# Last dense block reordered by feature halves, first routing moved forward, row splits moved to GpSimd, routing steps joined

## The chip, the cores and the metric

One core of a Trainium2 chip runs the whole program in one launch. The metric is device time in microseconds of one execution, the median over runs. Engines are named as the profile names them: PE (matrix products), PEld (its weight loads), DVE (vector), ACT (scalar), POOL (GpSimd), SP (the queue that issues most DMAs).

## The reference, cut to what matters

One decoder layer on 512 tokens of 1024 features. Up to the place of the change it computes a mixer and its residual; after it come two experts out of 32 for each token, a gated embedding and a last norm.

```
h = h + merged @ w_out[l]                 # the last dense block
u = rms_norm(h, norm_ffn_g[l])
group_logits = uf @ w_rg + b_rg;  g_idx = argmax(group_logits)
exp_logits = (uf @ w_re + b_re).reshape(n, 4, 8);  sel = exp_logits[g_idx]
top_v, top_i = lax.top_k(sel, 2)
gates = p_group * softmax(top_v)
y = silu(xblk @ w_gate_e[e]) * (xblk @ w_up_e[e]) @ w_down_e[e]   # per expert
```

## The kernel before, in words

Tokens lie in four tiles ("rows" i = 0 to 3) of 128 tokens. The dense products are made with values split into a high and a low part: for one k tile of 128 features the high weights take two products (high and low data) and the low weights one. A dense tile of 128 by 512 over eight k tiles is 24 products. The k tiles come in two halves, g = 0 and 1, of 12 products each. Fifteen dense blocks of four tiles run in turn; the last two, `out`, make `merged @ w_out` for columns 0 to 511 and 512 to 1023, and their tiles are the four rows. DVE adds each finished tile to `h1` (`residual`, L1197).

From the last block on, each row also needs the following work, and every engine's order is written out by hand:

- PE: `transpose_h1(i)` (8 transposes, L1529, two banks), `scores(i)` (16 recorded products with `wrt`, the router weights), `logits(i)` (a fold of two halves with `fold`).
- ACT: `row_norm(i)` (square sum and root, L887, L888), `copy_row_half` (PSUM to `h1T`, L895), `copy_scores` (L905), `row_high(i)` (the row's high part for the later gather, L901, which reads `h1` with a step of eight elements).
- DVE: `rows_split(i)` (the low part, `h1 - rows_high`, L439, same step), `row_rstd(i)`, and for two rows at a time `route(half)`: the logits with the bias (`lg`, L1221), then three times `first_max` (maximum, equality, index, minimum, one-hot: L1208 to L1214), once for the group and twice for the expert. `find_places(half)` turns the counts of the product `places(half)` into `pick` (L1250), the matrix that gathers tokens.
- PE then gathers the rows of the first team of experts with `pick` (`gather_k`, 32 products for rows 0 and 1 and 32 for rows 2 and 3), ACT copies them, and the expert loop begins with `gate_or_up`. `keep_busy(n)` (L1481) is n small products with no use of their result.

SP loads expert weights into nine slots of 2 MB. Slots 5 to 8 overlap the last block's operands: their first halves are loaded after `first_half_used`, their second halves after the last block's last tile (`tile_done`). Everything after the ninth load waits for slots to come free: first for `part_used`, which `gate_or_up` raises a quarter into its first run of products. The expert loop uses 96 such loads.

In the last block, tile c = 4 + i has row i - 1's transposes before its second k half, the scores inside that half and the logits behind it. `route(0)` stands on DVE before the last tile's `residual`, and row 3 (and its transposes, scores, logits) follows the block.

Of the kernel before, what the change touches and what calls it, by code (L numbers as in the profile page):

```python
# [37 lines left out]
def build(nc, x, p, norm_mix_g, w_in, conv_w, conv_b, w_rg, b_rg, w_ig, b_ig, lru_lambda, w_pool, pool_scale,  # L38
# [54 lines left out]
    with ctx:  # L93
# [131 lines left out]
        iota = sb("iota", [P, C])  # L225
        fold = sb("fold", [P, NL])
# [425 lines left out]
        def _(pool):  # L652
            steps = 0

            def after(ins):
# [17 lines left out]
                           allow_small_or_imprecise_dtypes=True).then_inc(const_ready, 1)  # L673
            nc.gpsimd.iota(token[:, :], pattern=[[P, TT]], base=-FAR, channel_multiplier=1,
                           allow_small_or_imprecise_dtypes=True).then_inc(const_ready, 1)
            nc.gpsimd.memset(row_base[:, :], float(FAR)).then_inc(const_ready, 1)
            pool.wait_ge(const_ready, 7)
# [35 lines left out]
            low(5)  # L713

# [25 lines left out]
        def _(act):  # L740
# [166 lines left out]
            for i in range(TT - 1):  # L907
                act.wait_ge(h1_ready, TT + i + 1)
                row_norm(i)
                if i > 0:  # L910
                    row_high(i)
                copy_row_half(i, 0)
                copy_row_half(i, 1)
                if i == 0:
                    row_high(i)
                copy_scores(i)
# [3 lines left out]
            copy_scores(TT - 1)  # L920
# [139 lines left out]
        def _(dve):  # L1060
# [31 lines left out]
            dve.wait_ge(const_ready, 7)  # L1092
# [113 lines left out]
            def first_max(scores, n, best, index, cands, onehot):  # L1206
# [9 lines left out]
            def route(half):  # L1216
# [6 lines left out]
                first_max(lg[:, at, 0:NG], NG, t4[:, 0, at], t4[:, 1, at], g4[:, 1, at, :], g4[:, 2, at, :])  # L1223

                el_g = el[:, at, :].rearrange("p i (g e) -> p i g e", g=NG)
                after(v.tensor_scalar(g4[:, 1, at, :], g4[:, 2, at, :], 2 * BIG, -BIG, ALU.mult, ALU.add))
                after(v.tensor_tensor(el_g, lg[:, at, NG:NL].rearrange("p i (g e) -> p i g e", g=NG),
                                      g4[:, 1, at, :].unsqueeze(3).to_broadcast([P, 2, NG, PG]), ALU.min))
                first_max(el[:, at, :], NE, t4[:, 2, at], t4[:, 3, at], cand[:, at, :], oh1[:, at, :])
                after(v.scalar_tensor_tensor(out=el[:, at, :], in0=oh1[:, at, :], scalar=-2 * BIG, in1=el[:, at, :],  # L1230
# [22 lines left out]
            for t, (kind, c) in enumerate(tiles):  # L1253
# [31 lines left out]
                if ("out", c) == (kind, 2 * TT - 1):  # L1285
                    route(0)
                if kind == "out":
                    if TT < c < 2 * TT - 1:
                        rows_split(dve, c - TT - 1)
                    residual(c)  # L1290
# [3 lines left out]
                    if c > TT:  # L1294
                        row_rstd(c - TT - 1)
            find_places(0)
            dve.wait_ge(rows_psum, 2 * TT)
            dve.wait_ge(scores_psum, TT - 2)
# [158 lines left out]
        def _(pe):  # L1457
            def mm(*a, **k):
                return nc.tensor.matmul(*a, **k)  # L1459
# [406 lines left out]
```

## Time and profile before

| what | value |
|---|---|
| median of 3 runs | 885.79 us (885.78 to 886.18) |
| profiled execution, span from first to last instruction | 884.5 us |
| PE busy | 836.7 us, 95% |
| PEld busy | 527.9 us, 60% |
| DVE busy | 342.2 us, 39% |
| ACT busy | 273.0 us, 31% |
| POOL busy | 82.1 us, 9% |
| moved by DMA | 253.85 MB, mean 287 GB/s |

The span belongs to one profiled execution; the median is of other executions of the same program and is 1.3 us higher. Busy shares are averages over stages with different limits: the dense blocks (0 to 348 us), the change-over to the experts (348 to 364), the expert loop (to about 813) and the last norm and gate.

### The profile page before, as it was taken

Reading aid. Unit: us, or ns where it says so; the run is one execution under the profiler, and the core shown is the slowest. Engines: PE = TensorE matmul, PEld = TensorE weight load, DVE = VectorE, ACT = ScalarE, POOL = GpSimd, SP = SyncE. Lnnn points to the kernel's source line nnn. Section 1 sums busy time; section 2 is a strip of 40 time slices with the busy share of each in tenths; the row PEclk is TensorE's granted clock in tenths of the full one; section 3 lists DMA queues with packets and bytes.
Section 4 is the critical chain, followed back from the end, with each engine's and each line's share of the span. In section 5 each row is a group of like instructions: output and inputs, shape, how many; then the busy total and the mean of one; then the engine's idle time right before and its main releaser. Section 6 shows DMA issues by size and latency. Waiting matters only on the chain.

```text
span 884.5 us, 10432 instructions
## 1 busy us (share of the span) xinstructions
PE 836.7 (95%) x4321; PEld 527.9 (60%) x4321; DVE 342.2 (39%) x479; ACT 273.0 (31%) x401; POOL 82.1 (9%) x64
## 2 busy tenths in 40 slices
PE   5999999999999999999999999888998898999996
PEld 4888888788888887536535354352352352533685
DVE  6899549962651616511020120101100101015865
ACT  7666346733332226202010100101001001002777
POOL 3436380000000000000000000000000000001000
PEclk9999999999999999999999999999899999999999
DMA  9222222211525764899999999999999999998902
GB/s 260 97 93 96 95 96 96 96 49 49 189 96 207 296 257 179 349 423 425 401 428 426 428 426 429 426 428 428 428 428 428 426 425 430 427 421 347 356 2 95
DMA packets 45334, 253.85 MB, mean 287 GB/s; under 512 B 8868, under 2 KB 9960, under 8 KB 31976
## 3 DMA queue, kind: packets, MB, share of 16 engines
q1 hardware_dynamic: 42696, 248.21, 69.2%
q0 software_dynamic: 2304, 4.20, 1.2%
q8 instruction: 34, 0.56, 0.3%
q10 hardware_dynamic: 288, 0.79, 0.2%
q14 instruction: 12, 0.10, 0.0%
HBM read 246.89 MB, written 10.49 MB: 291 GB/s over the span
## 4 chain that ended last, share of the span: by engine, by line
PE 44%; DMA 14%; issue 1%; DVE 1%; ACT 1%; DVEq 0%; ACTq 0%
PE bank L1459 42%; DMA ring<-in_w_down_e_dram 11%; DMA ring<-in_w_gate_e_dram 3%; PE bank L1689 1%; PE bank L1785 0%; ACT L1046 0%; ACT r_rounded L901 0%; PE bank L1529 0%; DVE pick L1250 0%; DVE r_rounded L439 0%; ACT r L999 0%; ACT L999 0%; ACT junk L887 0%; PE bank L1775 0%; ACT gain L895 0%
## 5 line engine op out<-in xcount | busy, mean ns | idle before, releaser
L1459 PE MATMUL bank<-ring_rounded,ring_rounded 128*128 128x512 f32 (+1 forms) x696 | 245.0, 389 | 0.3 <-DVE ring_rounded L1134 0.3
L1459 PE MATMUL bank<-r_rounded,ring_rounded 128*128 128x512 f32 (+1 forms) x744 | 234.4, 389 | 0.7 <-DVE ring_rounded L1081 0.6
L1459 PEld LDWEIGHTS bank<-r_rounded,ring_rounded 128*128 128x128 f32 x744 | 138.9, 188 | 30.4 <-DVE ring_rounded L1081 0.9
L1459 PEld LDWEIGHTS bank<-ring_rounded,ring_rounded 128*128 128x128 f32 x696 | 130.3, 188 | 28.1 <-issue 1.3
L1459 PE MATMUL bank<-ring,gain 128*64 128x512 f32 x472 | 118.0, 604 | 9.3 <-issue 8.1
L1459 PE MATMUL bank<-ring,hT 128*64 128x512 f32 x400 | 112.3, 624 | 6.7 <-DMA ring<-in_w_down_e_dram 6.7
L1459 PE MATMUL bank<-ring,junk 128*64 128x512 f32 x472 | 115.5, 592 | 0.0
L1459 PEld LDWEIGHTS bank<-ring,gain 128*64 128x64 f32 x472 | 36.1, 138 | 76.3 <-issue 73.5
L1459 PEld LDWEIGHTS bank<-ring,junk 128*64 128x64 f32 x472 | 37.6, 137 | 71.4 <-issue 71.3
L730 POOL DMA_INDIRECT expert_rows<-r,row_i x16 | 16.5, 1032 | 669.3 <-DVE r L1346 669.3
L945 ACT ACTIVATE r<-bank,factor 128x512 f32<-128x512 f32 x16 | 11.0, 687 | 215.2 <-PE bank L1459 215.2
L1459 PEld LDWEIGHTS bank<-pick,r_rounded 128*128 128x128 f32 x576 | 71.1, 195 | 9.3 <-issue 8.5
L1459 PE MATMUL bank<-pick,r_rounded 128*128 128x256 f32 x576 | 73.1, 288 | 3.3 <-DVE pick L1250 3.3
L1346 DVE TENSOR_SCALAR r<-bank,factor 128x512 f32<-128x512 f32 x16 | 12.0, 751 | 156.3 <-PE bank L1459 156.3
L418 DVE TENSOR_TENSOR ring_rounded<-ring,ring_rounded 128x2048 fp32r<-128x2048 f32 x21 | 49.0, 2343 | 54.5 <-ACT ring_rounded L413 54.5
L1459 PEld LDWEIGHTS bank<-ring,hT 128*64 128x64 f32 x400 | 34.8, 143 | 54.0 <-issue 49.3
L413 ACT ACTIVATE ring_rounded<-ring 128x2048 fp32r<-128x2048 f32 x28 | 53.4, 1912 | 37.2 <-DMA ring<-in_w_in_dram 12.5
L1459 PE MATMUL bank<-ring_rounded,r_rounded 128*128 128x512 f32 (+1 forms) x152 | 57.0, 379 | 0.0
L940 ACT ACTIVATE sig<-bank,factor 128x512 f32<-128x512 f32 x16 | 11.0, 687 | 131.7 <-PE bank L1459 123.9
L1336 DVE SCALAR_TENSOR_TENSOR sig<-bank,factor,sig 128x512 f32<-128x512 f32 x16 | 12.0, 750 | 100.0 <-ACT sig L940 100.0
L1340 DVE SCALAR_TENSOR_TENSOR sig<-bank,factor,sig 128x512 f32<-128x512 f32 x16 | 12.0, 751 | 96.2 <-PE bank L1459 96.2
L1459 PE MATMUL bank<-r,hT 128*64 128x512 f32 x80 | 37.0, 618 | 4.8 <-DMA ring<-in_w_down_e_dram 4.8
(226 smaller groups left out, 761.6 us busy)
## 6 DMA issues: line engine op xcount, KB each, us to landing
ring<-in_w_up_e_dram SPq DMA_DIRECT2D x29, 2048.0 KB, 29.6
ring<-in_w_gate_e_dram SPq DMA_DIRECT2D x24, 2048.0 KB, 27.9
ring<-in_w_down_e_dram SPq DMA_DIRECT2D x22, 2048.0 KB, 32.0
ring<-in_w_in_dram SPq DMA_DIRECT2D x18, 1024.0 KB, 7.3
r<-in_w_gate_e_dram SPq DMA_DIRECT2D x5, 2048.0 KB, 27.9
r<-in_w_down_e_dram SPq DMA_DIRECT2D x4, 2048.0 KB, 34.2
ring<-in_w_down_e_dram SPq DMA_DIRECT2D x7, 1024.0 KB, 21.6
ring<-in_w_up_e_dram SPq DMA_DIRECT2D x6, 1024.0 KB, 11.0
```

What stands on the lines that cost most here:

```text
L413: nc.scalar.activation(high_half(n, h), whole_half(n, h), ACT.Copy).then_inc(high_ready, 1)
L418: api.tensor_tensor(low_half(n, h), whole_half(n, h), high_half(n, h), ALU.subtract).then_inc(low_ready[low_engine[n, h]], 1)
L730: nc.gpsimd.indirect_dma_start(out=y_rows, out_offset=bass.IndirectOffsetOnAxis(ap=row_i[:, m:m + 1], axis=0), in_=yrow(m), in_offset=None ...
L940: nc.scalar.activation(sig[:, :], bank[2][:, :], ACT.Sigmoid, scale=factor[:, m, 1:2]).then_inc(sig_ready, 1)
L945: nc.scalar.activation(yrow(m)[:, HALF:D], y_bank(m, 1)[:, :], ACT.Copy, scale=factor[:, m, 0:1]).then_inc(y_stored, 1)
L1336: v.scalar_tensor_tensor(out=sig[:, :], in0=bank[2][:, :], scalar=factor[:, m, 1:2], in1=sig[:, :], op0=ALU.mult, op1=ALU.mult).then_inc(g ...
L1340: v.scalar_tensor_tensor(out=sig[:, :], in0=bank[3][:, :], scalar=factor[:, m, 1:2], in1=sig[:, :], op0=ALU.mult, op1=ALU.mult).then_inc(h ...
L1346: v.tensor_scalar(yrow(m)[:, 0:HALF], y_bank(m, 0)[:, :], factor[:, m, 0:1], None, ALU.mult).then_inc(y_stored, 1)
L1459: return nc.tensor.matmul(*a, **k)
L1689: ins = nc.tensor.transpose(bank[3][:, k * P:(k + 1) * P], sig[:, :].rearrange("p (q k) -> p k q", k=KF)[:, k, :], ident[:, :])
```

## The change

- **Last block.** It was row by row. Now row 0 and row 1 are whole; then come row 2's first k half, row 3's first k half, and only then the second halves of rows 2 and 3. Transposes and scores of rows 0 and 1 and both their logits stand inside the block; rows 2 and 3 follow it together. `first_half_used` is raised after row 3's first half.
- **First routing.** `route(0)` begins before row 2's `residual`, which is placed in the middle of it (`meanwhile`).
- **ACT.** The scores of rows 2 and 3 are copied by one instruction of 256 columns; `row_high(2)` and `row_high(3)` follow it.
- **Row splits.** All four `rows_split` leave DVE for POOL, each waiting for `rows_high_ready` and for the one before.
- **Routing.** `first_max` needs no index subtraction: a table `falling` (32, 31, ...) is multiplied by the equality in one `scalar_tensor_tensor` per row, so two instructions in a row without a wait between them replace two chained ones. The masking of the experts is joined the same way.
- **Filler.** `keep_busy` 6, 14 becomes 4, 4, around the first gather.

The diff, cut:

```diff
-        def rows_split(dve, i):
-            dve.wait_ge(rows_high_ready, i + 1)
-            dve.wait_ge(rows_psum, 2 * i)
-            nc.vector.tensor_tensor(rows_low(i), h1_by_k(i), rows_high(i), ALU.subtract).then_inc(rows_low_ready, 1)
...
+            for i in range(TT):
+                pool.wait_ge(rows_high_ready, i + 1)
+                if i >= 1:
+                    pool.wait_ge(rows_low_ready, i)
+                    pool.wait_ge(rows_psum, 2 * i)
+                nc.gpsimd.tensor_tensor(rows_low(i), h1_by_k(i), rows_high(i), ALU.subtract).then_inc(rows_low_ready, 1)
...
+            act.wait_ge(scores_psum, TT)
+            nc.scalar.activation(hT[0:64 + NL, 1:3, :],
+                                 bank[0][0:64 + NL, (TT - 2) * P:TT * P].rearrange("p (i t) -> p i t", i=2),
+                                 ACT.Copy).then_inc(scores_ready, 1)
+            row_high(TT - 2)
             row_high(TT - 1)
...
                 after(v.tensor_reduce(best, scores, AX.X, ALU.max))
-                after(v.tensor_tensor(cands, scores, bc(best, n), ALU.is_equal))
-                after(v.scalar_tensor_tensor(out=cands, in0=cands, scalar=-float(C),
-                                             in1=iota[:, 0:n].unsqueeze(1).to_broadcast([P, scores.shape[1], n]),
-                                             op0=ALU.mult, op1=ALU.add))
-                after(v.tensor_reduce(index, cands, AX.X, ALU.min))
-                after(v.tensor_tensor(onehot, cands, bc(index, n), ALU.is_equal))
+                for i in range(2):
+                    ins = v.scalar_tensor_tensor(out=cands[:, i, :], in0=scores[:, i, :], scalar=best[:, i:i + 1],
+                                                 in1=falling[:, NE - n:NE], op0=ALU.is_equal, op1=ALU.mult)
+                after(ins)
+                after(v.tensor_reduce(index, cands, AX.X, ALU.max))
+                after(v.tensor_tensor(onehot, cands, bc(index, n), compare))
...
-            find_places(0)
-            dve.wait_ge(rows_psum, 2 * TT)
-            dve.wait_ge(scores_psum, TT - 2)
-            v.tensor_copy(h1T(TT - 1)[:, 4:8, :],
-                          bank[4 + (2 * TT - 1) % 3][:, :].rearrange("p (k t) -> p k t", k=4)).then_inc(last_rows_ready, 1)
-            rows_split(dve, TT - 2)
+            for i in (TT - 2, TT - 1):
+                dve.wait_ge(rows_psum, 2 * i + 2)
+                dve.wait_ge(scores_psum, i - 1)
+                v.tensor_copy(h1T(i)[:, 4:8, :],
+                              bank[4 + (2 * i + 1) % 3][:, :].rearrange("p (k t) -> p k t", k=4)).then_inc(last_rows_ready, 1)
             find_places(0)
+            row_rstd(TT - 2)
             row_rstd(TT - 1)
             route(1)
...
             find_places(1)
-            rows_split(dve, TT - 1)
...
+            products(row2, 0)
+            transpose_h1(1)
+            bank_free(row3)
+            products(row3, 0).then_inc(first_half_used, 1)
+            scores(1)
+            logits(0)
+            logits(1)
+            products(row2, 1).then_inc(tile_done, 1)
+            products(row3, 1).then_inc(tile_done, 1)
...
+            transpose_h1(TT - 2)
             places(0)
             transpose_h1(TT - 1)
-            keep_busy(6)
+            scores(TT - 2)
             scores(TT - 1)
+            logits(TT - 2)
             logits(TT - 1)
+            keep_busy(4)
...
-            keep_busy(14)
+            keep_busy(4)
             places(1)
```

Three places show how instructions move. On PE, between the last dense product and the first gather, before (`ident` marks a transpose of a row, `wrt` the scores, `fold` the logits, `routed_bf` the counting products):

```order
L1459 MATMUL bank<-routed_bf,ones 128x32
L1529 MATMUL bank<-ident,r 128x128 [waits rows_ready,h1_ready]
L1529 MATMUL bank<-ident,r 128x128 x3
L1529 MATMUL bank<-ident,r 128x128 [waits rows_ready]
L1529 MATMUL bank<-ident,r 128x128 x3
L1459 MATMUL bank<-before,ones 128x128 x6
L1459 MATMUL bank<-gain,wrt 36x128 [waits rows_ready]
L1459 MATMUL bank<-gain,wrt 36x128 x3
L1459 MATMUL bank<-gain,wrt 36x128 [waits last_rows_ready]
L1459 MATMUL bank<-gain,wrt 36x128 x3
L1459 MATMUL bank<-fold,hT 128x36 [waits scores_ready]
```

and with the change, behind the transposes of rows 2 and 3:

```order
L1542 MATMUL bank<-ident,r 128x128 [waits rows_ready]
L1542 MATMUL bank<-ident,r 128x128 x3
L1472 MATMUL bank<-r,wrt 36x128 [waits rows_ready]
L1472 MATMUL bank<-r,wrt 36x128 x3
L1472 MATMUL bank<-r,wrt 36x128 [waits last_rows_ready]
L1472 MATMUL bank<-r,wrt 36x128 x3
L1472 MATMUL bank<-gain,wrt 36x128 [waits rows_ready]
L1472 MATMUL bank<-gain,wrt 36x128 x3
L1472 MATMUL bank<-gain,wrt 36x128 [waits last_rows_ready]
L1472 MATMUL bank<-gain,wrt 36x128 x3
L1472 MATMUL bank<-fold,hT 128x36 [waits scores_ready] x2
L1472 MATMUL bank<-before,ones 128x128 x4
```

Only row 3 was left behind the block; now rows 2 and 3 are, and their two logits wait for one copy.

On POOL, from the last dense block's weight splits to the read of the number of rounds, before and with the change:

```order
L710 TENSOR_TENSOR r<-r 128x512 [waits pool_step]
L418 TENSOR_TENSOR ring_rounded_53<-ring,ring_rounded_52 128x2048 [waits high_ready,pooled]
L418 TENSOR_TENSOR ring_rounded_53<-ring,ring_rounded_52 128x2048 [waits high_ready]
L716 TENSOR_LOAD rounds_i [waits rounds_ready]
L716 ISA x2
```

```order
L419 TENSOR_TENSOR ring_rounded_53<-ring,ring_rounded_52 128x2048 [waits high_ready,pooled]
L419 TENSOR_TENSOR ring_rounded_53<-ring,ring_rounded_52 128x2048 [waits high_ready]
L717 TENSOR_TENSOR r_rounded_60<-r,r_rounded_58 128x1024 [waits rows_high_ready]
L717 TENSOR_TENSOR r_rounded_57<-r,r_rounded_58 128x1024 [waits rows_psum,rows_low_ready,rows_high_ready] x3
L720 TENSOR_LOAD rounds_i [waits rounds_ready]
```

POOL gets four instructions of 128 by 1024 that wait for ACT, ahead of its read of the rounds.

On DVE, between the first `pick` and the experts' first maximum in `route(1)`, before:

```order
L1250 TENSOR_TENSOR pick<-iota,place 128x512 [waits dve_chain]
L1299 COPY gain<-bank 128x512 [waits scores_psum,rows_psum]
L439 TENSOR_TENSOR r_rounded_57<-r,r_rounded_58 128x1024 [waits rows_psum,rows_high_ready]
L1201 RECIPROCAL rstd<-std 128x1 [waits row_std_done]
L1221 SCALAR_TENSOR_TENSOR lg<-bank,rstd,brt 128x36 [waits logits_psum,dve_chain]
L1221 SCALAR_TENSOR_TENSOR lg<-bank,rstd,brt 128x36 [waits dve_chain]
L1208 TENSOR_REDUCE t<-lg 128x2 [waits dve_chain]
L1209 TENSOR_TENSOR g<-lg,t 128x8 [waits dve_chain]
L1210 SCALAR_TENSOR_TENSOR g<-g,iota 128x8 [waits dve_chain]
L1213 TENSOR_REDUCE t<-g 128x2 [waits dve_chain]
L1214 TENSOR_TENSOR g<-g,t 128x8 [waits dve_chain]
```

and with the change:

```order
L1264 TENSOR_TENSOR pick<-iota,place 128x512 [waits dve_chain]
L1211 RECIPROCAL rstd<-std 128x1 [waits row_std_done]
L1211 RECIPROCAL rstd<-std 128x1 [waits row_std_done,dve_chain]
L1231 SCALAR_TENSOR_TENSOR lg<-bank,rstd,brt 128x36 [waits logits_psum,dve_chain]
L1231 SCALAR_TENSOR_TENSOR lg<-bank,rstd,brt 128x36 [waits dve_chain]
L1218 TENSOR_REDUCE t<-lg 128x2 [waits dve_chain]
L1220 SCALAR_TENSOR_TENSOR g<-lg,t,falling 128x4 [waits dve_chain]
L1220 SCALAR_TENSOR_TENSOR g<-lg,t,falling 128x4
L1223 TENSOR_REDUCE t<-g 128x2 [waits dve_chain]
L1224 TENSOR_TENSOR g<-g,t 128x8 [waits dve_chain]
L1236 SCALAR_TENSOR_TENSOR sig<-g,lg 128x32 [waits dve_chain]
L1236 SCALAR_TENSOR_TENSOR sig<-g,lg 128x32
```

The row split between `pick` and the logits is gone, the copy of `h1T` has moved ahead, and each `first_max` has a pair without a wait inside it in the place of two waits.

## Rows read from the trace of the kernel before

**Rows 1.** Windows: stretch, length, busy time (count) of PE to POOL, clock, DMA share, GB/s.
```profile
346.00:364.00 18.00, 15.37 (x156) 13.48 (x154) 14.80 (x48) 7.36 (x14) 0.00 (x0) 1.00 1.01 423
364.00:366.00 2.00, 2.00 (x12) 0.63 (x10) 0.00 (x0) 1.73 (x5) 0.00 (x0) 1.00 0.23 94
540.00:800.00 260.00, 235.57 (x1266) 105.33 (x1264) 32.98 (x58) 26.65 (x57) 8.66 (x9) 0.96 1.01 427
```
**Rows 2.** Timeline of SP: start, duration, the first load that waits for `part_used`.
```profile
365.29 0.33 SPq L517 DMA_DIRECT2D ring<-in_w_down_e_dram  x1
```
**Rows 3.** Chain that ended last, from the last tile to the expert loop: start, us.
```profile
350.22 1.62 DVE r_rounded L439
...
352.39 0.27 DVE lg L1221
...
357.26 0.23 DVE routed_bf L1233
...
359.29 22.34 PE bank L1459 x143
```
**Rows 4.** Timeline of PE in the last block: transposes, scores, and a wait.
```profile
326.13 1.05 PE L1529 MATMUL bank<-ident,r 128*128 128x128 f32 x8
326.94 0.48 PE L1459 MATMUL bank<-ring_rounded,ring_rounded 128*128 128x512 f32 x1
...
328.96 1.07 PE L1459 MATMUL bank<-r,wrt 128*36 128x128 f32 x16
...
337.59 1.07 PE L1459 MATMUL bank<-gain,wrt 128*36 128x128 f32 x16 [0.72 <-ACT gain L895]
```
**Rows 5.** Timeline of DVE: the residuals of two tiles that follow each other.
```profile
318.17 0.69 DVE L1197 TENSOR_TENSOR r<-r,bank 128x512 f32<-128x512 f32 x1 [4.75 <-PE bank L1459]
323.61 0.69 DVE L1197 TENSOR_TENSOR r<-r,bank 128x512 f32<-128x512 f32 x1 [4.75 <-PE bank L1459]
```
**Rows 6.** Timeline behind the block: last scores' copy, first gather, two unchained DVE instructions.
```profile
351.04 0.28 ACT L905 ACTIVATE hT<-bank 100x128 f32<-100x128 f32 x1
351.62 4.07 PE L1459 MATMUL bank<-pick,r_rounded 128*128 128x256 f32 x32
...
357.54 0.17 DVE L1304 TENSOR_TENSOR g<-lg,t 128x16 f32<-128x16 f32 x1
...
357.63 0.15 DVE L1305 TENSOR_TENSOR t<-t 128x4 f32<-128x4 f32 x1
```
**Rows 7.** Timeline of POOL and DVE at two places early in the program.
```profile
16.12 4.58 POOL L418 TENSOR_TENSOR ring_rounded<-ring,ring_rounded 128x2048 fp32r<-128x2048 f32 x1 [10.97 <-ACT ring_rounded L413]
19.21 1.52 DVE L1096 TENSOR_SCALAR spt<-prm 128x8 f32<-128x8 f32 x1
...
28.29 4.62 POOL L418 TENSOR_TENSOR ring_rounded<-ring,ring_rounded 128x2048 fp32r<-128x2048 f32 x1 [7.59 <-ACT ring_rounded L413]
31.93 1.53 DVE L1134 TENSOR_TENSOR ring_rounded<-ring,ring_rounded 128x512 fp32r<-128x512 f32 x1 [0.70 <-ACT ring_rounded L798]
45.27 0.69 DVE L1134 TENSOR_TENSOR ring_rounded<-ring,ring_rounded 128x512 fp32r<-128x512 f32 x1
```
**Rows 8.** Groups by line and shape: names, shapes, count, busy us, mean ns.
```profile
L418 POOL TENSOR_TENSOR ring_rounded<-ring,ring_rounded 128x2048 fp32r<-128x2048 f32 x7 | 32.2, 4611 | 36.6 <-ACT ring_rounded L413 36.6
L901 ACT ACTIVATE r_rounded<-r 128x1024 fp32r<-128x1024 f32 x4 | 8.8, 2194 | 0.0
L887 ACT ACTIVATE junk<-r 128x1024 f32<-128x1024 f32 x4 | 4.2, 1056 | 22.4 <-DVE r L1197 22.4
```
**Rows 9.** Windows where PE stood idle in the expert loop.
```profile
576.00:578.00 2.00, 0.00 (x0) 0.00 (x0) 0.47 (x1) 0.00 (x0) 0.00 (x0) 1.00 1.00 426
...
616.00:618.00 2.00, 0.00 (x0) 0.00 (x0) 0.00 (x0) 2.00 (x6) 0.00 (x0) 0.88 1.02 434
...
624.00:626.00 2.00, 2.00 (x10) 0.63 (x8) 0.00 (x0) 0.00 (x0) 0.00 (x0) 0.91 1.06 451
...
754.00:756.00 2.00, 2.00 (x12) 2.00 (x11) 0.00 (x0) 0.00 (x0) 0.00 (x0) 0.51 0.99 420
```

More of the change, by code:

```diff
@@ L1222, in route @@
                                                  scalar=rstd[:, TT + i:TT + i + 1], in1=brt[:, :], op0=ALU.mult, op1=ALU.add))
[L1223 to L1228, printed above, removed]
+                first_max(lg[:, at, 0:NG], NG, t4[:, 0, at], t4[:, 1, at], g4[:, 1, at, :], g4[:, 2, at, :], ALU.not_equal)
+                for i in range(2 * half, 2 * half + 2):
+                    ins = v.scalar_tensor_tensor(out=el[:, i, :].rearrange("p (g e) -> p g e", g=NG),
+                                                 in0=g4[:, 2, i, :].unsqueeze(2).to_broadcast([P, NG, PG]), scalar=-2 * BIG,
+                                                 in1=lg[:, i, NG:NL].rearrange("p (g e) -> p g e", g=NG),
+                                                 op0=ALU.mult, op1=ALU.add)
+                after(ins)
                 first_max(el[:, at, :], NE, t4[:, 2, at], t4[:, 3, at], cand[:, at, :], oh1[:, at, :])
+                if meanwhile is not None:
+                    residual(meanwhile)
                 after(v.scalar_tensor_tensor(out=el[:, at, :], in0=oh1[:, at, :], scalar=-2 * BIG, in1=el[:, at, :],
@@ L1284, in _ @@
                                     ALU.mult).then_inc(wrt_ready, 1)
-                if ("out", c) == (kind, 2 * TT - 1):
-                    route(0)
                 if kind == "out":
-                    if TT < c < 2 * TT - 1:
-                        rows_split(dve, c - TT - 1)
-                    residual(c)
+                    if c == 2 * TT - 2:
+                        row_rstd(0)
+                        row_rstd(1)
+                        route(0, meanwhile=c)
+                    else:
+                        residual(c)
                     if c == TT:
@@ L1565, in places, with bank_free, products @@
                 ins.then_inc(places_psum, 1)
-            for t, (kind, c) in enumerate(tiles):
-                n = block_of[kind, c]
-                k_tiles = blocks[n][2]
-                dst = bank[t % 4][:, :]
+            def bank_free(t):
+                read_kind, read_c = tiles[t - 4]
+                pe.wait_ge(bank_read[read_kind], read_c + 1)
+            def products(t, g):
+                kind, c = tiles[t]
+                n = block_of[kind, c]
+                for part in ("high", "low"):
+                    for k in range(4 * g, 4 * g + 4):
+                        if t % 4 == 0 and k % 4 == 0:
+                            if part == "high":
+                                pe.wait_ge(high_ready, halves.index((n, g)) + 1)
+                            else:
+                                pe.wait_ge(*lows_at(n, g))
+                        if (kind, c, part) == ("out", 0, "high"):
+                            pe.wait_ge(merged_low_ready, k + 1)
+                        w = (high_half if part == "high" else low_half)(n, g)[:, k % 4, :]
+                        for factor, x_ in enumerate(moving[kind][0:2 if part == "high" else 1]):
+                            flags = dict(start=(k == 0 and part == "high" and factor == 0),
+                                         stop=(k == blocks[n][2] - 1 and part == "low"))
+                            if kind == "out":
+                                ins = mm(bank[t % 4][:, :], x_(k)[:, (c % TT) * P:(c % TT + 1) * P], w, **flags)
+                            else:
+                                ins = mm(bank[t % 4][:, :], w[:, (t % 4) * P:(t % 4 + 1) * P], x_(k), **flags)
+                return ins
+            LAST_BLOCK = len(tiles) - TT
+            for t, (kind, c) in enumerate(tiles[:LAST_BLOCK]):
                 if t == 3:
```

79 lines of the change are left out of this document (33 added, 46 removed).

## The prediction

> **What bounds the kernel now.** I read the windows first. From 540 to 800 us the DMA engines are full (share 1.01, 427 GB/s) while PE has idle time, so the expert loop ends when its weights have come in. In the window before the loop the engines are full as well, but from 364 to 366 their share falls to 0.23 [rows 1]: the slots are full, and the next load is issued only at 365.29 [rows 2], when PE has made the first quarter of the first expert's products. From then on the order of loads is fixed, so **what moves the start of that first product moves the end by as much**. Loads that start sooner than that only lengthen the gap at 364.
>
> The chain that ended last shows what sets that start [rows 3]: a row split on DVE (to 351.84), the second routing from 352.39, its one-hot sum at 357.26, and the second gather on PE at 359.29. From 357.26 to 359.29 (counting products, places, `pick`) nothing changes, and neither does what follows 359.29. So the sum below moves the 359.29.
>
> **The order of the last block.** A tile's 24 products take 5.44 us (323.61 less 318.17) [rows 5], 0.227 each. Transposes of a row cost PE 0.8 (326.13 to 326.94) and scores 1.07 [rows 4]. Row 1 begins at about 323.4, 0.2 before row 0's residual. From there to the last logits PE has 72 products (16.3), four transposes (3.2), four scores (4.3), logits and counts (0.9, an estimate at 0.15 each): 24.7. The wait at 337.59 for ACT's copy [rows 4] goes, since row 3's first half now lies between. New waits are one for ACT's copy of row 1's scores, 0.4 (it starts when the scores end and takes 0.28) [rows 6], and one of 0.5 for the joined copy, taken at 0.4 for twice the columns. The fold needs 0.6 from that copy's end until DVE can read it (before, the copy ended at 351.32 and the gather behind the fold started at 351.62) [rows 6]. 323.4 + 24.7 + 0.4 + 0.5 + 0.6 = 349.6. `route(1)` then starts there and not at 352.39: **-2.75**. 0.5 of it is the split that stood ahead of it [rows 3]; the rest is the removed wait and two rows handled in one pass instead of row 3 by itself. Row 2's residual inside `route(0)` and row 3's after it are ready before PE needs them: `route(0)` starts with row 1's logits at 323.4 + 5.44 + 0.8 + 1.07 + 2.72 + 0.8 + 2.72 + 1.07 + 0.7 = 338.7 and runs to about 344; the two second halves end at 338.9 + 5.44 = 344.3.
>
> **The joined routing steps.** Before, 20 chained steps lead from the first `lg` to the one-hot sum, 4.87 us in 20, 0.24 each [rows 3]. Four steps go (one in each `first_max`, one in the mask), 0.97, and four pairs each cost one more issue of 0.09 (357.54 to 357.63) [rows 6], 0.36: **-0.6** on the path. `route(0)` gets the same, but its result waits for PE.
>
> **The row splits on GpSimd.** ACT makes `row_high(2)` behind the joined copy, so from about 349.0 to 351.2 (2.19 each) [rows 8], and `row_high(3)` until 353.4. The two splits on POOL therefore start at about 351.2, 1.6 into `route(1)`, which still has some 2.8 us to go. Early in the program a DVE instruction on 8 columns that reads only SBUF took 1.52 us and ended at 20.73, POOL's split ended at 20.70. A DVE subtraction of two SBUF tensors took 1.53 where the same line takes 0.69 undisturbed, and ended 0.55 after POOL's instruction, which ended at 32.91 [rows 7]. So **a DVE instruction that meets a running POOL instruction stands still to its end**, and it is not shared by halves. Most of `route(1)` has two tensors in SBUF (the pairs, the one-hots, the masks); only the reductions do not. The first split holds DVE from the first expert pair on; when it ends, DVE gets one pair through, runs a reduction, and meets the second split. Each hold costs the split's length D less the reduction beside it, 0.3.
>
> D has no row. From below it is half of 4.61 [rows 8], 2.3, as though the step of eight cost nothing. ACT pays 2.19 for that pattern against 1.06 for the same size without a step [rows 8]; with the same factor POOL would need 4.7, with ACT's extra of 1.1 it needs 3.4. I take 2.8, between the contiguous row and the fixed extra, since POOL is already at over twice ACT's time for an element and part of a slower read may fall into that. Cost: 2 x (2.8 - 0.3) = **+5.0**; ends 2 x 2.0 = 4.0 and 2 x 4.4 = 8.8. PE's own need for the splits is later: both are done by 357.2.
>
> The rows show POOL at 2.25 ns an element without a step [rows 8]. The Trainium skill (GPSIMD Engine Reference, Performance pitfalls for Q7 kernels) says that a GpSimd loop which reads with a step above 8 bytes pays about one cycle more for an element. By that page D would be an estimated 3.15 and the hold cost 0.7 more; no run here shows it.
>
> The rows show holds only on a `tensor_scalar` and a `tensor_tensor` [rows 7]. The Trainium skill (SBUF — State Buffer, Who interferes with whom) says any VectorE instruction with two SBUF inputs contends with a GpSimd instruction that reads SBUF, and a reduction never does. By that page all of the pairs are held too; the traces agree as far as they go.
>
> **PE's clock.** Without the holds PE would come out of the first gather (32 products from 349.6 on, 4.07 long [rows 6], with eight fillers of 0.07) at 354.1, just as the one-hots are ready. With them it waits some 5 us, where two windows of the loop tell what happens: PE idle from 616 on, and the granted clock fell (0.88 in the window) to 0.5 and was back only within 624 to 626; another idle stretch, 576 to 578, kept 1.00; and a gather after an idle stretch ran at 0.51 [rows 9], the lower of the two levels, 1.2 GHz and not 2.4. After the idle window at 616 the low level ended only between 624 and 626. I take **+1.2**, some third of the second gather's 4 us of work at half speed; ends 0 and 2.8, two thirds of it.
>
> **The rest.** Fillers of 0.07 us that go shorten nothing, since PE waited behind them. The larger table costs one small POOL instruction at the start. SP's first-half loads leave some 5 us sooner, with no gain (above). POOL's read of the number of rounds comes behind the splits and is needed only for the first scatter, far later.
>
> **Sum.** -2.75 - 0.6 + 5.0 + 1.2 = +2.85. On the profiled execution's span that is 884.5 to 887.35; the median stands 1.3 us above the span, by which nothing changes, so 885.8 + 2.85 = **888.6**. With the ends of D and of the clock this case reaches from +0.65 (886.4) to +8.25 (894.0).
>
> **Rivals.**
> - **The splits don't hold DVE (faster).** If the small operands slip in between GpSimd's reads, the sum is -2.75 - 0.6 = -3.35: 882.4. For it: `route(1)`'s operands have 64 columns and fewer, and no row shows a broadcast operand held. Against it: 8 columns were held for 1.5 us [rows 7]. It turns into the forecast from the point where two holds cost more than 3.35, which is D = 2.0. Chance 0.17.
> - **One hold only.** The second split comes between DVE's instructions only after `route(1)`, or row 2's high part is made so much sooner that its split ends before the one-hots: -3.35 + 2.5 = -0.85, 884.9, with PE idle only half as long. For it: POOL waits for its own first result before its second instruction. Against it: that wait is far shorter than a pair and a reduction. Chance 0.13.
> - **GpSimd is far slower with the step.** With ACT's factor, D = 4.7: 885.8 - 3.35 + 8.8 + 1.2 = 892.4. Chance 0.12, inside the held case.
>
> **Numbers.** The held case has 0.70, with or without the long D. I leave out the unheld rival at the bottom (0.17) and the last of the long D, and take in the single hold: 884.3 to 892.5. About 0.2%, 1.8 us, is what a measurement of this kernel can tell from no change, so slower begins at 887.6. In the held case that needs D above 2.3 with the clock's 1.2, above 2.9 without it: 0.53 of the 0.70. Same: the other 0.17 and the single hold, 0.30. Faster: 0.17.
>
> **What would show it.** POOL's four instructions of 128 by 1024: their length is D. `lg` of rows 2 and 3 at 349.6. In `route(1)` two DVE instructions of over 2 us whose ends coincide with POOL's; if there are none, the forecast is wrong at that step and the time is near 882.4. The second gather at some 361 and not 359.29, with the granted clock under 1.00 in that window. The first load behind `part_used` at some 368. If `lg` does not come sooner, the reordering has failed and the time goes up by 2.75 more.

## The result and the profile after

The changed kernel takes 890.38 us (median of 9 executions, 889.8 to 892.01), the kernel before 887.24 (9 executions, 885.03 to 889.3). The ratio is **1.0040, 95% interval 1.0029 to 1.0051**: 3.5 us slower (2.6 to 4.5; the two medians differ by 3.1). The executions of the kernel before spread by 4 us, and their median stands 1.4 us above that of the three shown at first, which are among them, so differences and not levels are compared here. The profiled span went from 884.5 to 888.4, **+3.9** (forecast: +2.85).

The windows answer to [rows 1] (columns as there: stretch, length, busy time and count of PE, PEld, DVE, ACT, POOL, PE's clock, DMA share, GB/s).

```profile
358.00:360.00 2.00, 0.00 (x0) 0.00 (x0) 1.76 (x9) 0.00 (x0) 0.00 (x0) 0.50 0.51 213
360.00:362.00 2.00, 1.54 (x23) 1.49 (x23) 1.62 (x8) 0.31 (x2) 0.00 (x0) 0.50 0.06 16
362.00:364.00 2.00, 1.98 (x11) 1.76 (x9) 1.76 (x11) 0.00 (x0) 0.00 (x0) 0.50 0.00 0
364.00:366.00 2.00, 2.00 (x16) 2.00 (x16) 0.77 (x3) 0.00 (x0) 0.00 (x0) 0.81 0.00 0
540.00:800.00 260.00, 236.50 (x1272) 105.07 (x1270) 31.64 (x56) 24.47 (x50) 8.66 (x9) 0.96 1.01 427
```

From 540 to 800 nothing is different: DMA at 1.01 and 427 GB/s. Ahead of the expert loop the DMA engines, which before were full until 364, are all but empty from 360 on, since the loads into the last of the nine slots left sooner (their second halves from 344.80 on, before from 347.67) and no slot comes free. PE's clock is at 0.50, the lower of its two levels, from 358 to 364.

The chain that ended last shows what PE waits for (start, length, engine, what), beside [rows 3]:

```profile
349.94 0.27 DVE lg L1231
...
351.31 3.16 DVE g L1224
...
354.49 2.98 DVE sig L1236 x2
...
360.18 0.23 DVE routed_bf L1247
...
362.24 10.05 PE bank L1472 x53
```

The second routing starts 2.45 sooner (349.94, before 352.39), but its one-hot sum comes 2.92 later (360.18, before 357.26). In between stand two steps of 3 us on tensors of 8 and 32 columns. The timeline of DVE and POOL (start, length, engine, line, operation, names, shapes) shows what runs beside them, and the same two lines in the first routing, 10 us earlier:

```profile
340.85 0.17 DVE L1224 TENSOR_TENSOR g<-g,t 128x8 f32<-128x8 f32 x1
341.05 0.29 DVE L1236 SCALAR_TENSOR_TENSOR sig<-g,lg 128x32 f32<-128x32 f32 x2
...
351.27 6.14 POOL L717 TENSOR_TENSOR r_rounded<-r,r_rounded 128x1024 fp32r<-128x1024 f32 x2 [10.80 <-ACT r_rounded L905]
...
351.31 3.15 DVE L1224 TENSOR_TENSOR g<-g,t 128x8 f32<-128x8 f32 x1
354.49 2.97 DVE L1236 SCALAR_TENSOR_TENSOR sig<-g,lg 128x32 f32<-128x32 f32 x2
357.49 0.22 DVE L1218 TENSOR_REDUCE t<-sig 128x2 f32<-128x64 f32 x1
```

POOL's two splits fill 351.27 to 357.41, 3.07 each, so the first ends near 354.34. The two DVE steps end at 354.46 and 357.46, within 0.12 of each split's end, and take 2.98 and 2.68 more than undisturbed: 5.66. After that the routing runs on at its usual pace.

PE and SP, in the timeline, pass the delay on and add to it (in brackets the wait ahead of it and what ended it); compare [rows 6] and [rows 2]:

```profile
360.46 0.21 PE L1472 MATMUL bank<-routed_bf,before 128*128 128x32 bf16 x1 [6.29 <-DVE routed_bf L1247]
...
362.24 5.19 PE L1472 MATMUL bank<-pick,r_rounded 128*128 128x256 f32 x32
367.36 3.65 PE L1472 MATMUL bank<-ring,gain 128*64 128x512 f32 x16
```
```profile
369.34 0.33 SPq L512 DMA_DIRECT2D ring<-in_w_down_e_dram  x1
```

The gather starts 2.95 later and takes 5.19 where a gather took 4.07; the first load that waits for `part_used` leaves at 369.34, 4.05 later than at 365.29, and the span is 3.9 longer. The page's line of busy times shows why a sum of busy time would have misled:

```profile
PE 836.9 (94%) x4309; PEld 528.5 (59%) x4309; DVE 340.9 (38%) x476; ACT 272.4 (31%) x399; POOL 94.8 (11%) x69
```

Four splits of some 2.1 us (2.06 for the one at 350.22 in the kernel before) left DVE, yet DVE's busy time fell only from 342.2 to 340.9: an instruction that stands still counts as busy, and the holds put 5.66 back.

### The profile page after: what moved, and what is told of

The parts are those of the page before. It is cut to its first block, busy times and chain, and to the rows that moved or that the text cites. A ratio compares the mean times of both kernels' runs of the same rounds, so it can differ in the third digit from the quotient of the medians.

```text
span 888.4 us, 10408 instructions
## 1 busy us (share of the span) xinstructions
PE 836.9 (94%) x4309; PEld 528.5 (59%) x4309; DVE 340.9 (38%) x476; ACT 272.4 (31%) x399; POOL 94.8 (11%) x69
## 4 chain that ended last, share of the span: by engine, by line
PE 78%; DMA 16%; DVE 2%; issue 2%; ACT 2%; DVEq 0%; ACTq 0%
PE bank L1472 76%; DMA ring<-in_w_down_e_dram 14%; PE bank L1722 1%; DMA r<-in_x_dram 1%; DMA ring<-in_w_up_b_dram 1%; PE bank L1542 0%; ACT ring_rounded L414 0%; PE bank L1821 0%; DVE g L1224 0%; DVE sig L1236 0%; ACT L1056 0%; ACT junk L757 0%; DVE ring_rounded L1091 0%; ACT r_rounded L766 0%; PE bank L1485 0%
```

## The experiments

My theory was that of the forecast: the new order and the joined steps are worth some 3 us, and GpSimd's two late splits, which hold DVE, and the clock that falls while PE waits, cost more. The rivals: the joined instructions are slow by themselves; GpSimd has nothing to do with it; the loss arises elsewhere and the first load only shows it. The table has times in the trace, with each ratio to the kernel before. "One-hots" is the start of the one-hot sum (`routed_bf`), "first load" the first that waits for `part_used`; e2 leaves the low parts of rows 2 and 3 out of the gather, and in e8 these parts lie in another order.

| kernel | ratio (95%) | span | one-hots | second gather: start, length | first load |
|---|---|---|---|---|---|
| before | 1 | 884.5 | 357.26 | 359.29, 4.09 | 365.29 |
| changed | 1.0040 (1.0029, 1.0051) | 888.4 | 360.18 | 362.24, 5.19 | 369.34 |
| e1 splits after `pick` | 1.0019 (1.0010, 1.0028) | 887.5 | 354.54 | 359.62, 6.19 | 367.73 |
| e2 no late splits | 0.9966 (0.9954, 0.9979) | 881.4 | 354.32 | 356.34, 4.10 | 362.34 |
| e3 92 fillers | 1.0044 (1.0031, 1.0057) | 889.1 | 360.23 | 362.25, 5.58 | 369.74 |
| e9 114 fillers | 1.0024 (1.0015, 1.0033) | 887.2 | 360.05 | 362.08, 4.09 | 368.07 |
| e4 one late split | 1.0016 (1.0007, 1.0025) | 886.0 | 357.31 | 359.33, 5.51 | 366.75 |
| e8 no step | 1.0022 (1.0013, 1.0031) | 887.5 | 358.89 | 360.95, 5.49 | 368.35 |
| e7 old order, splits on GpSimd | 1.0041 (1.0026, 1.0057) | 887.9 | 359.32 | 361.35, 5.38 | 368.64 |
| e5 late splits on DVE | 0.9982 (0.9973, 0.9992) | 883.2 | 354.44 | 356.46, in two parts | 364.16 |
| e6 e5 with the old routing | 0.9993 (0.9982, 1.0005) | 883.9 | 355.08 | 357.10, 5.59 | 364.75 |
| e10 all splits on DVE | 0.9974 (0.9965, 0.9983) | 883.1 | 354.22 | 356.25, in two parts | 363.95 |

In all of them the span less the first load is 519.0 to 519.8 us. So nothing behind that load takes the delay back or adds to it by more than 0.8, and the last column can be read as the result. The ratios are of many executions and the spans of one each: beside e9, e10 and e11 the kernel before has a median span of 885.4, not 884.5, so for these three the ratio is the better measure of the gain or loss.

**e2: no late split in the way.**
```diff
+                if i == TT - 2:
+                    pool.wait_ge(info_made, 3)
...
-            pe.wait_ge(rows_low_ready, TT - 1)
...
-                gather_k(bank[4 + k // 2], k, TT - 2, start=False, stop=False)
+                gather_k(bank[4 + k // 2], k, TT - 2, (rows_high, rows_high), start=False, stop=False)
...
-            pe.wait_ge(rows_low_ready, TT)
...
-                ins = gather_k(bank[4 + k // 2], k, TT - 1, (rows_low,), start=False, stop=(k % 2 == 1))
+                ins = gather_k(bank[4 + k // 2], k, TT - 1, (rows_high,), start=False, stop=(k % 2 == 1))
```
Expected: 

> The changed kernel, with GpSimd's splits of rows 2 and 3 put behind the second routing and behind the gather; the gather of the first team leaves out the low parts of rows 2 and 3 (it multiplies their high parts in their place, so the count of products stays). This shows the changed order without any split in the way. Hold theory: one-hots near 354.5, the gather from 356.6 to 360.7, the load behind it 6.7 us sooner than in the changed kernel (near 362.6 instead of 369.3), and as every later transfer follows it, a span of 881.7, 2.8 below the kernel before. Rival (the load that is now sooner meets a busy ring or the later stages take it back): the load is sooner but the span falls by less than 5 us.

Measured, in the timeline of PE:

```profile
356.34 4.10 PE L1474 MATMUL bank<-pick,r_rounded 128*128 128x256 f32 x32 [0.62 <-DVE pick L1266]
```

One-hots at 354.32, gather from 356.34 to 360.44, first load 7.00 sooner than in the changed kernel and span 7.0 lower, ratio 0.9966. The rival (something later takes it back) falls. This is the value of order and joined steps with the splits' work left out of the path.

**e1: the splits after `pick`.**
```diff
+                if i == TT - 2:
+                    pool.wait_ge(pick_ready, 2)
```
Expected: 

> The changed kernel, with GpSimd's row splits 2 and 3 made to wait until VectorE has made the one-hots of the second half (after the second routing). Theory (the two splits held VectorE for 2.98 + 2.68 = 5.7 us in the second routing): the two held instructions fall back to about 0.17 and 0.3 us, the one-hots are made near 354.5 instead of 360.18; the second gather then waits for the splits themselves (two of 3.07 us after 356.5), ends near 364 instead of 367.4, and the load behind it starts 2.4 to 3.5 us sooner: profiled span 885 to 886 against 888.4. Rival (the joined instructions or their operands are slow by themselves, and GpSimd is not the cause): both instructions stay near 3 us, the one-hots stay near 360, and the later splits only add: 888.4 or more.

Measured: the two steps that were held are back at their usual length, 0.17 and 0.29 (first two lines below), and the one-hots come at 354.54, so the joined instructions are not slow by themselves. The hold went with the splits, to DVE steps behind `pick` that nobody waits for there (timeline of DVE, then of POOL):

```profile
351.31 0.17 DVE L1226 TENSOR_TENSOR g<-g,t 128x8 f32<-128x8 f32 x1
351.51 0.29 DVE L1238 SCALAR_TENSOR_TENSOR sig<-g,lg 128x32 f32<-128x32 f32 x2
...
356.64 0.15 DVE L1324 TENSOR_SCALAR rounds_i<-t 128x1 int32<-128x1 f32 x1
356.71 0.16 DVE L1327 TENSOR_REDUCE t<-g 128x4 f32<-128x16 f32 x1
356.90 2.60 DVE L1329 TENSOR_SCALAR t<-t 128x4 f32<-128x4 f32 x1
359.54 0.16 DVE L1330 TENSOR_TENSOR t<-t 128x4 f32<-128x4 f32 x1
359.74 0.18 DVE L1331 RECIPROCAL t<-t 128x4 f32<-128x4 f32 x1
359.95 2.55 DVE L1332 TENSOR_TENSOR t<-t 128x4 f32<-128x4 f32 x1
```
```profile
356.63 5.85 POOL L719 TENSOR_TENSOR r_rounded<-r,r_rounded 128x1024 fp32r<-128x1024 f32 x2 [16.16 <-DVE pick L1266]
```

The size was missed: 887.5 and not 885 to 886. PE waited 3.69 for the first split, its clock was at 0.50 from 358 to 364, and the gather took 6.19, not 4.

**e4: one late split instead of two.**
```diff
-            for i in range(TT):
+            for i in range(TT - 1):
...
             find_places(1)
+            rows_split(dve, TT - 1)
```
Expected: 

> The changed kernel, with the split of row 3 alone moved back to VectorE, behind the second routing; rows 0 to 2 stay on GpSimd. If each split holds VectorE once: one hold of 2.9 us is left in the second routing, one-hots near 357.5, the gather's load 2.9 to 3.8 us sooner than in the changed kernel, span 884.6 to 885.6. Rival (the hold has to do with the pair of splits back to back, and one alone holds nothing): one-hots near 354.5 and a span near 882.7. Rival (the hold has nothing to do with GpSimd): no change.

Measured, in the timeline of DVE:

```profile
351.12 3.13 DVE L1231 TENSOR_TENSOR g<-g,t 128x8 f32<-128x8 f32 x1
354.29 0.29 DVE L1243 SCALAR_TENSOR_TENSOR sig<-g,lg 128x32 f32<-128x32 f32 x2
```

One split, one hold (2.96); the second step is back at 0.29, and the one-hots come at 357.31 as expected. The pair back to back is not needed. The span, 886.0, misses the upper end by 0.4, since PE waited 3.60 for the counts and the gather took 5.51.

**e7: the splits alone, in the kernel before.**
```diff
-                    if TT < c < 2 * TT - 1:
-                        rows_split(dve, c - TT - 1)
...
-            rows_split(dve, TT - 2)
...
-            rows_split(dve, TT - 1)
```
with the four splits added on GpSimd as in the change. Expected: 

> The kernel before, in its own order and with its own routing, with only the four row splits moved from VectorE to GpSimd. Theory (each of GpSimd's splits holds one VectorE instruction for some 2.8 us when they meet): the split of row 2 meets the first routing or the residual behind it, that of row 3 the second routing; one hold of 2.9 us lies on the path, less some 0.5 us that VectorE saves, and perhaps 1 us of clock: 2.4 to 3.6 us above the kernel before. Rival (the changed order causes the loss and GpSimd's part costs nothing in the old order): no difference, or 0.5 us below.

Measured: ratio 1.0041, span 887.9, +3.4. The old order with the old routing loses as much as the changed kernel does, and for the same reason (timeline of DVE, then of POOL):

```profile
343.14 0.22 DVE L1215 TENSOR_REDUCE t<-sig 128x2 f32<-128x64 f32 x1
343.39 2.90 DVE L1216 TENSOR_TENSOR sig<-sig,t 128x64 f32<-128x64 f32 x1
...
353.17 3.03 DVE L1233 TENSOR_SCALAR g<-g 128x8 f32<-128x8 f32 x1
```
```profile
343.17 3.04 POOL L720 TENSOR_TENSOR r_rounded<-r,r_rounded 128x1024 fp32r<-128x1024 f32 x1 [4.92 <-ACT r_rounded L908]
353.12 3.04 POOL L720 TENSOR_TENSOR r_rounded<-r,r_rounded 128x1024 fp32r<-128x1024 f32 x1 [6.92 <-ACT r_rounded L908]
```

The second routing starts 0.8 sooner (351.59, before 352.39) since no split stands ahead of it, loses 2.86 to one hold, and the gather, at 5.38, gives 1.3 more to the clock: +3.35, which is the first load's delay. The first hold lies in the first routing; in spite of it the second one starts sooner.

**e8: the split without its step.** GpSimd's splits of rows 2 and 3 read `h1[:, i, :]` in its own order.
```diff
-                nc.gpsimd.tensor_tensor(rows_low(i), h1_by_k(i), rows_high(i), ALU.subtract).then_inc(rows_low_ready, 1)
+                nc.gpsimd.tensor_tensor(rows_low(i), h1_by_k(i) if i < TT - 2 else h1[:, i, :].rearrange("p (k q) -> p k q", k=KD),
+                                        rows_high(i), ALU.subtract).then_inc(rows_low_ready, 1)
```
Expected: 

> The changed kernel, with GpSimd's splits of rows 2 and 3 reading their first operand in consecutive elements instead of with a step of 32 bytes (the low part of these rows then has its elements in another order, which changes what is computed, not its amount). If the step makes the split long: 2.3 us (as GpSimd's nearest row of the kernel before per element) instead of 3.07, each hold 0.75 us shorter, span 1.5 us below the changed kernel. Rival (the step costs nothing on this engine): 3.07 us each and no difference.

Measured, POOL's timeline and then DVE's:

```profile
351.23 4.89 POOL L717 TENSOR_TENSOR r_rounded<-r,r_rounded 128x1024 fp32r<-128x1024 f32 x2 [10.78 <-ACT r_rounded L906]
```
```profile
351.30 2.37 DVE L1225 TENSOR_TENSOR g<-g,t 128x8 f32<-128x8 f32 x1
353.70 2.46 DVE L1237 SCALAR_TENSOR_TENSOR sig<-g,lg 128x32 f32<-128x32 f32 x2
```

2.45 a split instead of 3.07, and the held steps shorter by 0.78 and 0.51, together twice that difference: the one-hots come 1.29 sooner. The hold follows the length of GpSimd's instruction. The span gains 0.9 of that and not the 1.5 expected, as the gather was 0.3 slower here.

**e3 and e9: the clock.** The filler in the wait ahead of the second gather is made longer.
```diff
-            keep_busy(4)
+            keep_busy(92)
             places(1)
```
(114 in e9.) Expected of 92: 

> The changed kernel, with the filler products ahead of the second gather raised from 4 to 92 (some 6.4 us more of them, in the 6.3 us in which TensorE waits for the one-hots). Theory (1.1 us of the loss is TensorE's clock, at 0.50 from 358 to 364): the granted clock stays at 1.00, the gather's 32 products take 4.07 instead of 5.19 us, and the span is 887.2, 1.1 to 1.3 below the changed kernel; the held VectorE instructions stay at 3 us each. Rival (the clock falls for another reason, or the gather's length is not its clock): no change. If the filler runs past the one-hots it costs what it runs over, under 0.5 us.

Expected of 114: 

> The changed kernel with 114 filler products in place of 4 (92 were too few: they ended at 359.1, TensorE then waited 1.4 us, and the gather ran at half clock all the same). They now end near 360.4, where the one-hots come at 360.2. Theory (the low clock of the second gather follows TensorE's idle time ahead of it): granted clock 1.00 from 358 to 366, the gather 4.1 us instead of 5.2, span 887.3 against 888.4. Rival (the clock falls all the same, since TensorE's short waits for the places behind the one-hots, which the kernel before has too, are enough there): the gather stays above 5 us, span 888.4 to 889.1.

Measured with 92 (timeline of PE, then windows):

```profile
353.78 5.31 PE L1472 MATMUL bank<-before,ones 128*128 128x128 bf16 x92
360.51 0.19 PE L1472 MATMUL bank<-routed_bf,before 128*128 128x32 bf16 x1 [1.42 <-DVE routed_bf L1247]
```
```profile
360.00:362.00 2.00, 1.12 (x23) 0.95 (x23) 1.66 (x8) 0.31 (x2) 0.00 (x0) 1.00 0.04 16
362.00:364.00 2.00, 1.75 (x9) 1.75 (x10) 1.76 (x11) 0.00 (x0) 0.00 (x0) 0.65 0.00 0
364.00:366.00 2.00, 2.00 (x12) 2.00 (x11) 0.78 (x3) 0.00 (x0) 0.00 (x0) 0.50 0.00 0
```

A miss: the filler ended at 359.09, PE waited 1.42, and the clock fell later but fell: gather 5.58. With 114 (timeline of PE, then windows):

```profile
353.65 6.54 PE L1472 MATMUL bank<-before,ones 128*128 128x128 bf16 x114
...
362.08 4.09 PE L1472 MATMUL bank<-pick,r_rounded 128*128 128x256 f32 x32 [0.62 <-DVE pick L1264]
```
```profile
362.00:364.00 2.00, 1.92 (x16) 1.92 (x17) 1.75 (x11) 0.00 (x0) 0.00 (x0) 1.00 0.03 8
364.00:366.00 2.00, 2.00 (x19) 1.96 (x17) 0.63 (x2) 0.51 (x2) 0.00 (x0) 1.00 0.00 0
```

The clock stays at 1.00, the gather takes 4.09, and the span is 887.2, 1.2 below the changed kernel; holds and one-hots are as there. So with PE's wait for the counts filled (it still waits 0.62 for `pick`) the clock stayed up, and the clock is 1.1 of the loss.

**e5, e11, e6, e10: what is left without the holds.** In e5 the splits of rows 2 and 3 stand on DVE behind `find_places(1)`, and PE gathers both high parts before the low ones; e10 has the other two on DVE as well.
```diff
             find_places(1)
+            rows_split(dve, TT - 2)
+            rows_split(dve, TT - 1)
...
                         row_rstd(1)
+                        rows_split(dve, 0)
+                        rows_split(dve, 1)
                         route(0, meanwhile=c)
```
(the last two added lines in e10 alone). Expected of e5: 

> The changed kernel, with the splits of rows 2 and 3 back on VectorE behind the second routing (rows 0 and 1 stay on GpSimd), and TensorE gathering both high parts first, then the low part of row 2, then of row 3. Theory (without a hold the new order is worth its 2.45 us and the joined routing some 0.3): one-hots near 356.5 at the latest, gather's end near 361.7, the load behind it 5.7 us sooner than in the changed kernel, span 882.7: about 1.8 below the kernel before and 5.7 below the changed one. Rival (the splits on VectorE, some 1.1 us each, now stand in the way of the gather): span 884.5, equal to the kernel before.

Of e6, which has the old routing steps: 

> The variant with the last two splits on VectorE (the run before this one), with the routing steps written as in the kernel before (a compare and a multiply-add on the whole half in place of one joined instruction for each row; the mask in two steps). This tells what the joined steps alone are worth, without a hold in the way. By the prediction's term 0.6 us longer, by the trace of the changed kernel (the pair that replaced them costs 0.41 where one instruction had been counted) 0.3 us longer, both on the path once; rival: joined steps gain nothing, no difference.

Of e11, which is e5 again: 

> The variant with the last two splits on VectorE once more, beside the one that has all four there, to compare the two on one chip: 1.5 to 2 us below the kernel before if its first result holds (ratio 0.998), and its second gather again at a granted clock of 1.00.

Of e10: 

> The variant with the last two splits on VectorE, with the first two moved there as well (ahead of the first routing), so that nothing is left on GpSimd: the new order and the joined routing alone. If GpSimd's splits of rows 0 and 1 are worth nothing there: the same time as the variant with two, within 0.5 us (VectorE stands idle from 332.3 to 339.3, but the split of row 1 ends some 0.2 us after the first logits come, against 0.1 us that GpSimd's split holds the first routing). Rival (they free VectorE where it is wanted): over 0.5 us slower than that variant.

Measured: e5 883.2, faster than both kernels (ratio 0.9982, and 0.9981 when repeated as e11), though it takes back only part of what e2 shows, above all because the last 8 products wait for the second split (timeline of e5):

```profile
356.32 4.26 DVE L441 TENSOR_TENSOR r_rounded<-r,r_rounded 128x1024 fp32r<-128x1024 f32 x2
...
360.63 1.21 PE L1481 MATMUL bank<-pick,r_rounded 128*128 128x256 f32 x8 [0.91 <-DVE r_rounded L441]
```

e6 is slower than e5 by 0.64 at the one-hots and 0.59 at the first load. Only 0.29 of that lies in the second routing (4.88 from `lg` to the one-hots, against 4.59); the other 0.35 is that PE now waits for the residual behind the first routing (timeline of e6):

```profile
345.93 1.16 PE L1549 MATMUL bank<-ident,r 128*128 128x128 f32 x8 [0.33 <-DVE r L1214]
```

e10, with nothing on GpSimd, is no slower than e11 on the same chip (884.98 and 885.10 us, spans 883.1 and 883.4), and its ratio, **0.9974 (0.9965 to 0.9983)**, is the lowest but for e2's, which leaves work out: 2.3 us below the kernel before and 5.9 below the changed one by the ratios. Its interval overlaps that of e11 (0.9972 to 0.9990). GpSimd's splits of rows 0 and 1, which held nobody for long, were worth nothing either: DVE stood idle from 332.3 to 339.3 in the changed kernel and had room for the first two.

## Why the prediction was right, point by point

- **What sets the end: right.** A delay of the first gate product is passed on whole: 4.05 at the first load, 3.9 in the span, and in the twelve kernels of the table within 0.8.
- **The new order: right, a little too good.** `lg` came at 349.94, forecast 349.6: -2.45 instead of -2.75. The wait for the joined copy was 0.48 (taken: 0.5); from the fold's start to `lg` it took 0.74 where 0.6 was taken for it; the rest of the miss lies ahead of that copy.
- **The joined steps: half the size.** From `lg` to the one-hots the changed kernel takes 10.24; less the 5.66 of the holds that is 4.58, against 4.87 before: -0.29, forecast -0.6. The step that failed is the price of a pair: one more issue of 0.09 was taken from two small steps [rows 6], but the pairs on the experts take 0.41 against 0.22 for one instruction, and that on the groups 0.36 against 0.17: 0.19 more each. With 0.06 for the mask's pair (0.29 against 0.23) the four pairs cost 0.63 where 0.36 was taken. That the first routing's gain "waits for PE" held with the joined steps, but with little room: e6 shows that the old ones would have made PE wait 0.33.
- **The holds: right in kind and number, near in place.** Two, each to the end of a split. They fell on the one-hot of the groups and on the masking, three and two steps ahead of the expert pair that was named: the first split started when forecast (351.27, named 351.2), and `lg` 0.34 later than forecast. No pair came through between the splits and no reduction ran beside them, as the forecast has it: the second step stood still 0.03 after the first had ended. D was 3.07 (taken 2.8). The part that was not lost, 0.24 a hold, is near the 0.3 that was taken, but by luck: it is not a reduction, but about the undisturbed length of the held steps themselves (0.17 and 0.29). DVE lost 5.66 (taken 5.0). The step of eight costs 0.62 of D (e8: 2.45 without), so contiguous 1024 elements take a little more than half of the 2048-element row [rows 8].
- **The clock: right in kind, its size in part luck.** +1.1 (gather 5.19 against 4.09), taken 1.2 from ends of 0 and 2.8, and e9 shows that it is this. But the cost does not grow with the wait: PE waited 6.29 for the counts here and the gather lost 1.1; in e4 it waited 3.60 and the gather lost 1.4; in e1 it waited 3.69 for the split and the gather lost 2.1. In the changed kernel the clock stood at 0.50 from 358, 4 us before the gather began, and rose within 364 to 366; in e4 it fell within 358 to 360 (0.80), where the gather began, and stood at 0.50 from 360 to 362. So after the longer wait more of the low stretch had passed before there was work.
- **The sum.** -2.45 - 0.29 + 5.66 + 1.1 = +4.0, forecast +2.85, and the span measured +3.9. The sum missed by some 1.2: 0.3 of the order, 0.3 of the pairs and 0.66 of the holds, less 0.1 of the clock. The level (888.6 against 890.38) is off by 0.6 more, most of it because the profiled execution stands 1.8 above its own span (890.18 for 888.4), where 1.3 was taken from a median and a span of different executions. The signs that were named came so: the gather moved from 359.29 to 362.24 (named: some 361), the first load to 369.34 (some 368).
- **The rivals.** "No hold" is e2: forecast -3.35, measured -3.1 in the span with the late splits out of the path. "One hold only" is e4: forecast -0.85, measured +1.5; the parts of that miss are the clock, which was left out there as PE would be "idle only half as long" (gather 5.51, 1.4 more), a hold of 2.96 where 2.5 was taken, and the order and pairs (0.6). "Far slower with the step" fell: 3.07 and not 4.7.

The Trainium skill (SBUF — State Buffer, Who interferes with whom) says that a VectorE instruction with two SBUF inputs contends with a GpSimd instruction that reads SBUF, and that a reduction never does. The traces agree: the `scalar_tensor_tensor` pair was held for 2.68, and the reduction at 356.71 in e1 took 0.16 beside a running split. The Trainium skill, in the same section, also counts `tensor_scalar` among those that can contend, and the trace agrees there too (3.03 at 353.17 in e7).

The Trainium skill's extra cycle for each element of a read with a long step (GPSIMD Engine Reference, Performance pitfalls for Q7 kernels) gave an estimate of 3.15 for D. Measured was 3.07, but from 2.45 and not 2.3, so the step cost 0.6 ns an element here and not the 0.83 of that estimate.

Open: why PE's clock fell in e6 (0.83 from 356 to 358, 0.50 from 358 to 360) and stayed at 1.00 in e5. Their waits ahead of the gather are nearly the same (0.62 for the counts and 0.62 for `pick` in e5, 0.93 and 0.62 in e6). The length of these waits alone does not decide it, since the kernel before waited longer and its clock stayed at 1.00 (timeline of PE):

```profile
355.53 0.96 PE L1459 MATMUL bank<-before,ones 128*128 128x128 bf16 x14
357.55 0.19 PE L1459 MATMUL bank<-routed_bf,before 128*128 128x32 bf16 x1 [1.06 <-DVE routed_bf L1233]
...
359.29 4.09 PE L1459 MATMUL bank<-pick,r_rounded 128*128 128x256 f32 x32 [0.63 <-DVE pick L1250]
```

It has 14 fillers ahead of that wait where e5 and e6 have 4, and no run changes that number alone. Each of these clocks is that of one execution: e6's spans run from 883.7 to 887.2, e5's from 882.6 to 883.7, so it may differ from one execution to the next, which is not shown. So e6 against e5 prices the joined steps at the one-hots, not in the span.

## What to carry to other kernels

Work that is moved from VectorE to GpSimd can still stop VectorE while it runs: ask which VectorE instructions will meet it (here `tensor_tensor`, `scalar_tensor_tensor` and `tensor_scalar` on SBUF were held, even on 4 columns, and reductions were not), and charge nearly one full GpSimd instruction for each meeting that lies on the path. Here 2.1 us of VectorE's own time was traded for a hold of 2.7 to 3.0; the same splits done by VectorE itself, where it is idle or behind the step that others wait for (e10, which also gathers the high parts first), turned a loss of 0.40% into a gain of 0.26%. A wait on the path can be paid a second time, in the clock of the products behind it: look at the granted clock after every new wait of PE.

## What the runs showed of the hardware that was not expected

- Splits back to back hold VectorE almost without a break: in the changed kernel the step that had waited ended at 354.46 and the very next one stood still from 354.49; in e1 one `tensor_tensor` (359.54) came through between the two.
- Not every VectorE instruction is held: beside a running split a reciprocal took 0.18 (e1, 359.74), a reduction 0.16 (e1, 356.71), and in the first routing of the changed kernel the logits from PSUM (339.32) their usual 0.55, while 4 columns of `tensor_scalar` took 2.60. The `tensor_scalar` at 356.64 in e1 started with the split and was not held.
- Filler that took 5.31 of the 6.7 us between PE's first gather and the counts bought nothing, and filler that took all but 0.14 of it bought 1.2: in e3 the clock was still at 1.00 in the stretch where PE waited and fell in the one behind it, under the gather itself. That is one profiled execution; e3's six spans run from 887.5 to 890.9.
